# Stacked operands and values in a chunked RWKV-7 scan on one Trainium2 core

## The chip, the cores and the metric

The kernel runs on one core of one Trainium2 chip. The metric is the time of one execution on the device in microseconds (us); the median of the timed runs stands for a kernel. All data are float32.

## The reference

The program is a two-layer hybrid diffusion backbone: 256 latent and 256 context tokens of 1024 channels. Each layer has a Fourier mix, a latent attention, a bidirectional RWKV-7 recurrence, a gated merge, and a mixture of experts. The change concerns the recurrence alone:

```python
def wkv_scan(r, w, k, v, a, b, S0, reverse):
    def step(S, inp):
        rt, wt, kt, vt, at, bt = inp
        sa = jnp.einsum('bhvk,bhk->bhv', S, at)
        S = S * wt[:, :, None, :] + sa[..., None] * bt[:, :, None, :] + vt[..., None] * kt[:, :, None, :]
        return S, jnp.einsum('bhvk,bhk->bhv', S, rt)
...
    for d in range(2):
        ...
        s_fin, yd = wkv_scan(rh, decay, kd, vh, -kk, kk * a, S0[d], reverse=(d == 1))
        ys.append(yd)
...
y_ctx, s_ctx = rwkv_mix(pr_c, zero_state, *rw)
y_lat, _ = rwkv_mix(pr_l, s_ctx, *rw)
```

There are 8 heads of 64 channels and two directions d (0 forward, 1 backward). The context is scanned first, then the latent tokens from the context's last state. In the second (last) layer nobody reads the context's output y, only its state.

## The kernel before

**Layout.** Two heads share the 128 partitions (h = 0 in partitions 0 to 63, h = 1 in 64 to 127), and four such pairs j = 0 to 3 lie beside each other, so one head is a 64x64 block and one operand of a direction a 128x256 tile. PSUM has 8 banks of 128x512; the helper `part(d, n, x)` is half x of bank 4d+n.

**Steps.** A chunk is 64 tokens. A layer's scan has `STEPS` = 8 steps: k = 0 to 3 are the context, k = 4 to 7 the latent tokens, and each step handles one chunk of either direction. `streams(l, k)` says that y is wanted: always in layer 0, in layer 1 only for k of 4 and more. In a step a chunk's recurrence is a triangular system: `couple` makes its 64x64 matrix from keys and decays; `begin` masks it (MT) and starts the inverse X and its transpose XT with 2x2 blocks (negated neighbours plus the unit diagonal); five levels n = 0 to 4 double the blocks, each by `join` (BT times X into PSUM), a ScalarE copy to PS (L1254), `grow` (XT times PS), and on VectorE an add and a 32x32-block transpose (L1619, L1621). `grams` makes the masked score matrices Grb, Grk, Gak; `turns` transposes keys (Bt, Kt), `values` transposes the chunk's values (Vt), by products with an identity block.

**The chunk before.** What depends on the state runs one step late, between the pieces of the inverse: `correct(k-1)` makes the right-hand side, `solve(k-1)` U = X^T RHS, `readout(k-1)` the output, `update(k-1)` the new state.

**Order.** The order on each engine is written out by hand. TensorE in step k: couple(k), correct(k-1), grams(k, 0), solve(k-1), grams(k, 1), then the levels; turns(k) stand in level 0, readout(k-1) in levels 1 and 2, update(k-1) in level 3, values(k+1) in level 4. VectorE: begin and masks, the running sums of the decays for k+1 (`cumulate`), then per level the add and transpose of both directions, `operands(k+1, d)` in levels 1 and 2, `read` (y += readout) there too, `totals` and `update` in level 3. ScalarE copies PSUM to SBUF and takes the exponentials; GpSimd (POOL) multiplies MT by each level's mask (`blocks`, L1914) and subtracts and multiplies for the decays.

**Names.** L731 is the single matmul line of all scan products. L1590 is the last operand of `couple`; L1596 to L1600 are `begin`; L1607, L1608, L1611 the masks; L1624 the last add of level 4; L1639 and L1640 the state's add and its product with the total decay; L1220 the copy of the turned keys, L1225 of the values, L1230 of the right-hand side, L1235 of U. In the trace a float32 product of the program is two matmul records, a transpose through TensorE one.

The loop over the levels, on TensorE:

```python
for n in range(len(LEVELS)):
    join(k, n, 0)
    ...
    join(k, n, 1)
    ...
    grow(k, n, 0)
    grow(k, n, 1)
```

## Time and profile before

| | |
|---|---|
| Median of 3 runs | 2350.64 us (2346.11 to 2356.69) |
| The profiled execution's own time | 2349.85 us |
| Its span in the trace | 2348.2 us |
| TensorE busy | 2101.7 us (90%) |
| VectorE, ScalarE, GpSimd busy | 720.6, 487.9, 274.7 us |
| Scan of layer 0, first couple to last readout | 420.4 to 620.8 us |
| Scan of layer 1, the same | 1625 to 1819 us |
| Matmuls of L731 | 11520 records |

Busy time counts an engine as busy while any of its instructions is in flight. A scan matmul is in flight for some 0.22 us and the next begins long before it ends, so a busy TensorE can still have room; the distance between starts is the measure there. PEclk is the share of full clock that TensorE was granted: 1.00 is 2.4 GHz, 0.50 is 1.2 GHz.

### The profile page before, as it was taken

To read this page: it belongs to the slowest core of one execution; us is meant where nothing else is said; L and a number is where in the kernel's file an instruction comes from. 1 tells how busy PE (TensorE), PEld (TensorE's weight loads), DVE (VectorE), ACT (ScalarE), POOL (GpSimd) and SP (SyncE) were. 2 spreads that over 40 slices of the span, in tenths; PEclk is the share of its full clock that TensorE was granted. 3 is DMA by queue.
4 is the path that set the end of the run, shared out by engine and by line. 5 is a ranking of instruction groups with operands and counts; after the bars stand their busy time and mean duration, and the time that the engine had idled before them with its cause. 6 is when DMAs were issued, how large, how long until landed. Compare 5 with 4: busy or idle time off the path is not lost. (4 is left out here: it accounts for less than half of the span.)

```text
span 2348.2 us, 53901 instructions
## 1 busy us (share of the span) xinstructions
PE 2101.7 (90%) x23898; PEld 1349.7 (57%) x23898; DVE 720.6 (31%) x1768; ACT 487.9 (21%) x1120; POOL 274.7 (12%) x463
## 2 busy tenths in 40 slices
PE   6999899899899999999999789898999899987784
PEld 2454443889644444446556465554898788754442
DVE  1033334777431011310100032546676311200002
ACT  2123312333220000301111132323332301110011
POOL 0000000443100001101111100001343000011111
PEclk8999999899999999999999989998899999998996
DMA  7148716000121212448999821110000344799993
GB/s 287 61 154 344 305 65 226 3 4 4 56 90 54 108 54 108 181 161 328 398 383 395 306 90 51 69 50 1 4 4 4 146 159 188 274 378 397 395 406 122
DMA packets 55828, 399.91 MB, mean 170 GB/s; under 512 B 6672, under 2 KB 22928, under 8 KB 33648
## 3 DMA queue, kind: packets, MB, share of 16 engines
q1 hardware_dynamic: 43440, 361.94, 39.9%
q0 software_dynamic: 8576, 23.08, 2.6%
q10 hardware_dynamic: 3648, 12.45, 1.7%
q8 instruction: 134, 2.20, 0.4%
q14 instruction: 30, 0.25, 0.0%
HBM read 365.47 MB, written 31.98 MB: 169 GB/s over the span
## 5 line engine op out<-in xcount | busy, mean ns | idle before, releaser
L494 PE MATMUL ps<-H,memory 128*128 128x512 f32 (+2 forms) x1728 | 615.1, 512 | 11.6 <-DMA memory<-in_w_in 9.7
L494 PEld LDWEIGHTS ps<-H,memory 128*128 128x128 f32 (+1 forms) x1728 | 327.5, 190 | 286.5 <-issue 251.6
L731 PE MATMUL ps<-memory 64*64 64x32 f32 (+2 forms) x10112 | 329.0, 229 | 33.6 <-DVE memory L1624 10.1
L994 PE MATMUL ps<-memory 128*32 128x256 f32 x5120 | 298.8, 395 | 49.2 <-DMA memory<-in_eu 47.7
L731 PEld LDWEIGHTS ps<-memory 64*64 64x64 f32 x10112 | 316.4, 142 | 43.3 <-issue 21.3
L494 PE MATMUL ps<-memory 128*128 128x512 f32 (+3 forms) x928 | 319.2, 495 | 6.2 <-issue 3.0
L994 PEld LDWEIGHTS ps<-memory 128*32 128x32 f32 x5120 | 184.8, 114 | 160.0 <-issue 71.0
L494 PEld LDWEIGHTS ps<-memory 128*128 128x128 f32 (+1 forms) x928 | 173.8, 188 | 143.6 <-issue 127.3
L1019 PE MATMUL ps<-memory 128*32 128x256 f32 x2560 | 144.8, 380 | 5.0 <-ACT memory L1342 3.8
L1914 POOL TENSOR_TENSOR memory<-memory,cons 128x256 f32<-128x256 f32 x160 | 117.9, 752 | 122.5 <-DVE memory L1596 78.7
L1019 PEld LDWEIGHTS ps<-memory 128*32 128x32 f32 x2560 | 79.6, 110 | 59.9 <-ACT memory L1342 10.1
L1979 POOL DMA_DIRECT2D expert_rows<-memory x128 | 69.3, 542 | 299.1 <-DVE memory L1846 276.4
L1278 ACT ACTIVATE memory<-ps 128x512 f32<-128x512 f32 (+1 forms) x48 | 23.6, 491 | 329.3 <-PE ps L494 329.3
L1714 DVE TENSOR_TENSOR memory<-memory,ps 128x512 f32<-128x512 f32 (+1 forms) x32 | 17.8, 555 | 209.6 <-PE ps L494 209.6
L1254 ACT COPY memory<-ps 128x128 f32<-128x128 f32 x160 | 43.0, 269 | 173.2 <-PE ps L731 173.2
L731 PE MATMUL ps<-cons,memory 64*64 64x64 f32 x1408 | 59.2, 233 | 13.5 <-issue 10.5
L731 PEld LDWEIGHTS ps<-cons,memory 64*64 64x64 f32 x1408 | 52.0, 146 | 16.5 <-issue 12.2
L1841 DVE TENSOR_TENSOR memory<-memory,ps 128x256 f32<-128x256 f32 x16 | 6.7, 421 | 174.3 <-ACT memory L1340 174.3
L1619 DVE TENSOR_TENSOR memory<-memory,ps 128x128 f32<-128x128 f32 x128 | 34.4, 269 | 78.4 <-PE ps L731 78.2
L1621 DVE STREAM_TRANSPOSE memory<-memory 128x256 f32<-128x256 f32 x128 | 57.0, 445 | 4.4
L1846 DVE COPY memory<-ps 128x256 f32<-128x256 f32 x32 | 13.6, 424 | 137.8 <-PE ps L1019 137.8
L1952 POOL TENSOR_TENSOR memory<-H 128x512 f32<-128x512 f32 (+1 forms) x2 | 2.0, 993 | 436.1 <-ACT H L1288 436.1
(251 smaller groups left out, 1804.9 us busy)
## 6 DMA issues: line engine op xcount, KB each, us to landing
memory<-in_eg SPq DMA_DIRECT2D x32, 2048.0 KB, 17.2
memory<-in_eu SPq DMA_DIRECT2D x32, 2048.0 KB, 23.0
memory<-in_ed SPq DMA_DIRECT2D x32, 2048.0 KB, 23.4
memory<-in_w_ada SPq DMA_DIRECT2D x24, 2048.0 KB, 9.5
memory<-in_w_in SPq DMA_DIRECT2D x20, 2048.0 KB, 7.6
expert_rows<-memory SPq DMA_DIRECT2D x4, 3456.0 KB, 23.7
memory<-in_w_out SPq DMA_DIRECT2D x4, 2048.0 KB, 7.8
memory<-expert_rows ACTq DMA_DIRECT2D x19, 384.0 KB, 10.4
```

Of the source, the lines that this page charges most:

```text
L494: ins = mm(ps[0:M, bank, 0:w], lhs(k), rhs(k), start=(k == 0), stop=(k == n - 1))
L731: ins = mm(out[cols, j], lhs[rows, j, :], rhs[rows, j], start=(n == 0), stop=(n == len(terms) - 1))
L994: ins = mm(out_.rearrange("p (x n) -> p x n", x=2), XGT[:, k, g * GROUP:g * GROUP + GROUP], sets[b][:, 0:2, k * 512 + c * P:k * 512 + c * ...
L1019: ins = mm(ps[cc, 6 if last else 5, at:at + 256], HIDT[:, 0, g * P + k * GROUP:g * P + k * GROUP + GROUP], sets[b][:, 2, k * D + c * 256:k ...
L1254: act.copy(under(PS[n][d], n, d), under(part(d, 3, 0).rearrange("p (j n) -> p j n", n=CH), n, d))\
L1278: act.activation(SG[:, o % 2, 0:w], ps[:, 2 * (o % 2), 0:w], ACT.Sigmoid).then_inc(sem("merge_sigmoid"), 1)
L1619: tt(x, x, under(half(d, 2, 1 - p), n, d), ALU.add).then_inc(sem("inverse"), 1)
L1621: dve.transpose(flat(TWICE["XT"][p][d]), flat(ONCE["X"][d])).then_inc(sem("inverse"), 1)
L1714: link(tt(TM[:, 0, 0:w], gate, proj, ALU.mult))
L1846: dve.tensor_copy(YG[:, b, (groups - 1) * 256:groups * 256], ps[:, 6, 0:256]).then_inc(sem("result_copied"), 1)
L1914: tt(BTS[n][d], ONCE["MT"][d], over_pairs(con_(f"lev{LEVELS[n]}")), ALU.mult).then_inc(sem("blocks"), 1)
L1979: pool.dma_start(xg[bass.ds((2 * i + b) * tr, tr), c * 256:c * 256 + 256] .rearrange("(g t) n -> t g n", t=GROUP), YG[GROUP * c:GROUP * c ...
```

## The change

- **Stacked operands.** The two operands of the keys lie side by side per pair (`BB`), so that one matmul with 128 stationary columns makes what two made (`grams`), and one transpose turns both (`turns`). These are now true TensorE transposes, no longer products with an identity.
- **Stacked values.** U and the values V share one tile `UV` of 128 partitions (64 of U, 64 of V for each head), as do their score matrices (`GR`) and keys (`BK`). `readout` and `update` contract over 128 rows, and two products become one. V is transposed once for both directions (`pick`, `VC`).
- **Order.** `correct` is split in two; on TensorE `solve` now stands behind grams(k, 1), the turns move to level 1, both readouts to level 2, both updates stand together in level 3, and the values behind the levels. Bank numbers change (`bank`).
- **ScalarE** takes over three things: it writes the unit diagonal into XT a step ahead (`diagonals`), so that VectorE's begin is a mask, a predicated copy and a transpose; it multiplies the state by the total decay in four pieces of 128x64 per direction (`decayed_state`); it copies y at the first visit of a chunk (`first_read`), so that GpSimd no longer zeroes Y. Signs are moved (`B` is negated at its making) so that no copy has to negate.

```diff
+        GR = [[pairs(piece(2)) for d in range(2)] for p in range(2)]
+        UV = [pairs(piece(2)) for d in range(2)]
+        BB = [pairs(piece(2)) for d in range(2)]
+        GAK = pairs(piece(2))
+        VC = pairs(piece(2))
...
+                def values(k):
+                    pe.wait_ge(sem("values_moved"), picked(l * STEPS + k))
...
+                            ins = pe.transpose(ps[:, bank(h, 3), 256 + CH * j:256 + CH * j + CH], VC[side(h), j], eye[side(h), :])
...
                 def grams(k, d):
...
-                    pe.wait_ge(sem("values_held"), nth(N, d))
+                    if k:
+                        pe.wait_ge(sem("state"), states(l, k - 1, d))
...
+                            ins = mm(ps[:, bank(d, h), 128 * j:128 * j + CH * wide], BB[d][side(h), j], ER[p][d][side(h), 0:wide, j],
+                                     start=True, stop=True)
...
+                            ins = pe.transpose(ps[:, bank(d, h), CH * j:CH * j + CH], BB[d][side(h), j], eye[side(h), :])
...
+                def correct_values(k):
+                    N = l * STEPS + k
+                    for d in both:
+                        pe.wait_ge(sem("masked"), nth(N, d))
+                        pe.wait_ge(sem("values_moved"), held(N, d))
...
+                    for j, d, h in problems:
+                        mm(part(d, 1, 0)[side(h), j], ONCE["S"][d][side(h), j], ER[p][d][side(h), 1, j], start=(j == 0), stop=False)
+                    for j, d, h in problems:
+                        ins = mm(part(d, 1, 0)[side(h), j], UV[d][:, j, h], GR[p][d][:, j, h], start=False, stop=(j == RJ - 1))
...
                     if n == 0 and k:
-                        pe.wait_ge(sem("u_copied"), nth(N - 1, d))
+                        pe.wait_ge(sem("u_copied"), nth(N - 1, 1))
...
                 def solve(k):
                     for d in range(2):
                         act.wait_ge(sem("u"), nth(l * STEPS + k, d))
-                        act.copy(flat(ONCE["U"][d]), part(d, 3, 1)).then_inc(sem("u_copied"), 1)
+                        rows = side(d)
+                        act.copy(by_head(UV[d])[rows], quarters(rows, slice(bank(0, 3), bank(1, 3) + 1), 1)[:, ::-1 if d else 1]).then_inc(sem("u_copied"), 1)
+
+                def diagonals(k):
+
+                    for d in range(2):
+                        act.copy(TWICE["XT"][k % 2][d], over_pairs(con_("eye")))
...
+                def decayed_state(k, d):
+
+                    act.wait_ge(sem("state_added"), carried(l, k, d))
+                    for j in range(RJ):
+                        x = ONCE["S"][d][:, j]
+                        ins = act.activation(x, x, ACT.Identity, scale=total[:, k % 3, d, j:j + 1])
+                    ins.then_inc(sem("state"), 1)
...
-                    link(tt(turned, half(d, 2, p), over_pairs(con_(f"pair{1 - d}")), ALU.mult))
-                    link(tt(turned, turned, over_pairs(con_("eye")), ALU.add))
+                    dve.wait_ge(sem("exps"), grown(N, d))
+                    link(dve.copy_predicated(turned, over_pairs(con_(f"pair{1 - d}")).bitcast(mybir.dt.uint32), half(d, 2, p)))
...
-                    link(tt(state, state, half(d, 0, 0), ALU.add))
-                    tt(state, state, total[:, k % 3, d, :].unsqueeze(2).broadcast_to([P, RJ, CH]), ALU.mult)\
-                        .then_inc(sem("state"), 1)
+                    tt(state, state, half(d, 0, 0), ALU.add).then_inc(sem("state_added"), 1)
...
-                pool.memset(Y[:, :, :], 0.0)
```

The front of a step on TensorE, before. Rows are matmuls of the program, output shape behind the names; the 64x2x64 rows are the wide half of grams, and the last row is join(k, 0, 0).

```order
L731 MATMUL ps<-memory 64x64 [waits keys,inverse]
L731 MATMUL ps<-memory 64x64 x15
L731 MATMUL ps<-memory 64x64 [waits state,masked,values_held]
L731 MATMUL ps<-memory 64x64 x31
L731 MATMUL ps<-memory 64x64 [waits queries,read,values_held]
L731 MATMUL ps<-memory 64x64 x7
L731 MATMUL ps<-memory 64x2x64 x8
L731 MATMUL ps<-memory 64x64 [waits rhs_copied,inverse]
L731 MATMUL ps<-memory 64x64 x15
L731 MATMUL ps<-memory 64x64 [waits queries,read,values_held]
L731 MATMUL ps<-memory 64x64 x7
L731 MATMUL ps<-memory 64x2x64 x8
```

Behind them stands join(k, 0, 0), which waits for u_copied, inverse and blocks. The same place in the changed kernel (L775 couple, L817 and L827 the two halves of correct, L800 grams, L838 solve, L875 join):

```order
L775 MATMUL ps<-memory 64x64 x15
L817 MATMUL ps<-memory 64x64 [waits masked,values_moved]
L817 MATMUL ps<-memory 64x64 x15
L800 MATMUL ps<-memory 128x128 [waits queries,read,state]
L800 MATMUL ps<-memory 128x128 x7
L827 MATMUL ps<-memory 64x64 [waits state,values]
L827 MATMUL ps<-memory 64x64 x15
L800 MATMUL ps<-memory 128x128 [waits queries,read,state]
L800 MATMUL ps<-memory 128x128 x7
L838 MATMUL ps<-memory 64x64 [waits rhs_copied,inverse]
L838 MATMUL ps<-memory 64x64 x15
L875 MATMUL ps<-memory 64x16x2 [waits u_copied,inverse,blocks]
```

Solve moved behind the second grams and now touches the join that waits for its copy, and the product after couple now waits for copied values.

ScalarE from the end of level 4 into the next step, before (L1254 level copies, L1225 values, L1230 right-hand side, L1197 log decays, L1235 U):

```order
L1254 COPY memory<-ps 128x4x32 [waits joined] x2
L1225 COPY memory<-ps 128x256 [waits values] x2
L1230 ACTIVATE memory<-ps 128x256 [waits rhs] x2
L1197 COPY memory<-memory 128x256 [waits rhs] x2
L1235 COPY memory<-ps 128x256 [waits u] x2
```

And in the changed kernel (L1357 level copies, L1333 the decayed state, L1305 values, L1316 U, L1321 the diagonals):

```order
L1357 COPY memory<-ps 128x4x32 [waits joined] x2
L1333 ACTIVATE memory<-memory,total 128x64 [waits state_added]
L1333 ACTIVATE memory<-memory,total 128x64 x3
L1333 ACTIVATE memory<-memory,total 128x64 [waits state_added]
L1333 ACTIVATE memory<-memory,total 128x64 x3
L1305 COPY memory<-ps 64x2x4x64 [waits values]
L1305 COPY memory<-ps 64x2x4x64
L1310 COPY memory<-ps 128x256 [waits rhs] x2
L1265 COPY memory<-memory 128x256 [waits rhs] x2
L1316 COPY memory<-ps 64x2x4x64 [waits u] x2
L1321 COPY memory<-cons 128x256 x2
```

Eight small activations now stand ahead of the values' copies, and those copies and U's have 512 elements per partition, on 64 partitions, where they had 256 on 128.

## Rows read from the trace of the kernel before

**Rows 1.** The page, part 1: busy us (share of the span), instructions.
```profile
PE 2101.7 (90%) x23898; PEld 1349.7 (57%) x23898; DVE 720.6 (31%) x1768; ACT 487.9 (21%) x1120; POOL 274.7 (12%) x463
```

**Rows 2.** Windows, one scan step each; columns are named in the first row.
```profile
core 0: us, PE busy (x) PEld busy (x) DVE busy (x) ACT busy (x) POOL busy (x), PEclk, DMA share, GB/s
442.50:466.50 24.00, 22.78 (x768) 22.36 (x769) 18.01 (x48) 8.11 (x26) 10.21 (x14) 1.00 0.02 5
...
541.50:567.00 25.50, 22.84 (x768) 22.41 (x769) 18.21 (x48) 8.11 (x26) 10.21 (x14) 1.00 0.02 5
591.10:612.40 21.30, 20.30 (x672) 19.65 (x673) 13.65 (x38) 3.99 (x14) 7.37 (x11) 0.99 0.02 4
1649.70:1674.30 24.60, 22.94 (x640) 22.17 (x641) 16.78 (x42) 8.12 (x26) 8.80 (x12) 0.79 0.01 4
1674.30:1695.90 21.60, 19.07 (x644) 18.16 (x645) 16.80 (x42) 8.10 (x26) 8.80 (x12) 1.00 0.02 4
1744.00:1768.00 24.00, 22.73 (x781) 22.24 (x781) 17.98 (x48) 8.10 (x26) 10.21 (x14) 1.00 0.02 4
```

**Rows 3.** Windows of L731 alone: a couple, and a level without other work.
```profile
567.02:567.50 0.48, 0.48 (x31) 0.48 (x33) 1.00 0.00 0
1682.74:1685.17 2.43, 2.43 (x64) 2.24 (x65) 1.00 0.02 7
```

**Rows 4.** Timeline of TensorE at three places: start us, us, what, [idle before].
```profile
499.68 1.15 PE L731 MATMUL ps<-cons,memory 64*64 64x64 f32 x32 [0.26 <-issue]
...
164.82 0.66 PE L668 MATMUL ps<-cons,memory 128*128 128x128 f32 x4
165.41 1.09 PE L649 MATMUL ps<-memory 128*64 128x128 f32 x8
...
982.17 2.30 PE L941 MATMUL ps<-memory,cons 128*128 128x16 f32 x20
```

**Rows 5.** Groups of ScalarE by form: out<-in xcount | busy us, mean ns | idle before.
```profile
L1220 ACT COPY memory<-ps 128x512 f32<-128x512 f32 x28 | 16.4, 586 | 26.1 <-PE ps L731 26.1
...
L1225 ACT COPY memory<-ps 128x256 f32<-128x256 f32 x32 | 11.0, 373 | 0.7 <-PE ps L731 0.7
...
L1303 ACT ACTIVATE memory<-ps 128x64 f32<-128x64 f32 x1 | 0.2, 242 | 0.0
```

**Rows 6.** Groups of VectorE by form.
```profile
L1599 DVE TENSOR_TENSOR memory<-memory,cons 128x256 f32<-128x256 f32 x32 | 23.1, 722 | 1.1
L1640 DVE TENSOR_TENSOR memory<-memory,total 128x256 f32<-128x256 f32 x28 | 18.0, 642 | 1.0
...
L1598 DVE TENSOR_TENSOR memory<-ps,cons 128x256 f32<-128x256 f32 x32 | 13.1, 410 | 0.0
...
L1639 DVE TENSOR_TENSOR memory<-memory,ps 128x256 f32<-128x256 f32 x28 | 11.4, 407 | 0.0
...
L1714 DVE TENSOR_TENSOR memory<-memory,ps 128x512 f32<-128x512 f32 x16 | 11.0, 688 | 140.3 <-PE ps L494 140.3
```

**Rows 7.** Timeline of VectorE and TensorE, end of one step and the next couple.
```profile
589.81 0.73 DVE L1640 TENSOR_TENSOR memory<-memory,total 128x256 f32<-128x256 f32 x1
590.47 0.47 DVE L1624 TENSOR_TENSOR memory<-memory,ps 128x128 f32<-128x128 f32 x2
...
591.08 0.33 PE L731 MATMUL ps<-memory 64*64 64x64 f32 x6 [0.84 <-DVE memory L1624]
```

**Rows 8.** Windows around two falls of TensorE's clock.
```profile
1639.50:1642.90 3.40, 2.88 (x91) 2.71 (x87) 3.33 (x10) 1.06 (x4) 1.92 (x4) 1.00 0.02 5
1642.90:1649.70 6.80, 6.32 (x124) 6.21 (x120) 2.47 (x10) 1.23 (x5) 0.00 (x0) 0.50 0.01 2
...
1707.80:1711.20 3.40, 2.29 (x76) 2.30 (x74) 3.33 (x9) 0.85 (x3) 1.08 (x2) 1.00 0.00 0
1711.20:1714.60 3.40, 3.40 (x72) 3.40 (x69) 0.60 (x2) 0.27 (x1) 0.00 (x0) 0.50 0.03 7
```

**Rows 9.** The zeroing of Y, from the groups of GpSimd.
```profile
L1897 POOL MEMSET memory<- 128x2048 f32 x2 | 3.6, 1804 | 227.2 <-DVE marks L1376 227.2
```

More of the change, by code:

```diff
@@ L766, in turns @@
+                    ins.then_inc(sem("grams"), 1)
                 def turns(k, d):
                     pe.wait_ge(sem("masked"), nth(l * STEPS + k, d))
-                    heads(None, (part(d, 0, 0), (ONCE["bE2"][d], eye, 0, 0)))
-                    heads("turns", (part(d, 0, 1), (ONCE["bKk"][d], eye, 0, 0)))
-                def correct(k):
+                    for j in range(RJ):
+                        for h in both:
+                            ins = pe.transpose(ps[:, bank(d, h), CH * j:CH * j + CH], BB[d][side(h), j], eye[side(h), :])
@@ new lines, in update @@
+                def update(k):
+                    N, p = l * STEPS + k, k % 2
+                    for d in both:
+                        pe.wait_ge(sem("u_copied"), nth(N, d))
+                        pe.wait_ge(sem("masked"), nth(N + 1, d))
+                        if k + 2 < STEPS:
+                            pe.wait_ge(sem("turned"), carried(l, k + 1, d))
+                    for j, d, h in problems:
+                        ins = mm(part(d, 0, 0)[side(h), j], BK[p][d][:, j, h], UV[d][:, j, h], start=True, stop=True)
+                        if j == RJ - 1 and h:
+                            ins.then_inc(sem("step"), 1)
@@ L804, in join, with heads @@
+                def heads(signal, made, lhs, rhs, d):
+                    for j in range(RJ):
+                        for h in both:
+                            at = side(h ^ d)
+                            ins = mm(made[at, j], lhs[at, j], rhs[at, j], start=True, stop=True)
+                    ins.then_inc(sem(signal), 1)
                 def join(k, n, d):
@@ L1240, in _ @@
                     growths(0, d)
+                for d in range(2):
                     decays(0, d)
-                values(0)
                 for k in range(STEPS):
@@ L1250, in _ @@
                         solve(k - 1)
+                        if more:
+                            diagonals(k + 1)
                     for n in range(len(LEVELS)):
@@ L1255, in _ @@
                                .then_inc(sem("joined_copied"), 1)
-                            if n == 0 and more:
+                        if more and n == 1:
+                            for d in range(2):
                                 turns(k, d)
-                        if more and n in (1, 2):
-                            decays(k + 1, n - 1)
                         if more and n < 2:
@@ L1262, in _ @@
                             growths(k + 1, n)
-                    if more:
-                        values(k + 1)
+                        if more and n == 2:
+                            for d in range(2):
+                                decays(k + 1, d)
+                        if n == 2:
+                            pick(k)
+                        if n == 3 and k and first(k - 1) and streams(l, k - 1):
+                            for d in range(2):
+                                first_read(k - 1, d)
+                    if k:
+                        for d in range(2):
+                            decayed_state(k - 1, d)
+                    values(k)
                 correct(STEPS - 1)
@@ L1626, in read @@
                 def read(k, d):
-                    if streams(l, k):
+                    if streams(l, k) and not first(k):
                         dve.wait_ge(sem("readout"), 2 * readouts(l, k) - 1 + d)
```

221 lines of the change are left out of this document (123 added, 98 removed).

## The prediction

> **What bounds the kernel now.** I read the busy shares first: TensorE is in flight 90% of the span, no other engine over 31% [rows 1]. The change touches the scan alone, so I cut it into steps [rows 2]. A middle step of layer 0 takes 24.0 to 25.5 us; its six middle steps fill 442.5 to 591.1 us, 24.8 us each. They hold 768 matmuls, 18 us of VectorE, 8 of ScalarE, 10 of GpSimd. TensorE sets the end, though "busy" hides how full it is, so I price its matmuls by the distance between starts.
>
> - Where the blocks lie on the array's diagonal (h stays h: levels, readout, update), two run at a time: 32 products in 1.15 us, 0.22 of it the last one's flight, so 29 ns each [rows 4].
> - Where all four quarters are used (couple, correct, solve), 31 take 0.48 us: 15 ns [rows 3].
> - Loading 128 stationary columns sets 107 ns even when 16 columns are streamed: 20 in 2.30 us with 0.26 of flight [rows 4]. Two such on different row halves make 53 ns. The wide scores of before also stream 128 columns, 53 ns.
>
> Before, a full step has 128 records at 15 ns (1.9 us), 32 wide ones at 53 ns (1.7) and 608 at 29 ns (17.6): 21.2 us. So 3.6 us of 24.8 are waits: a level's own chain (64 records are 1.87 us, an unfilled level takes 2.43 [rows 3]) and the end of the step, where couple waits 0.84 us for VectorE's last add, which itself starts only after the state's product [rows 7].
>
> **What TensorE loses in work.** After, a full step has 128 records at 15 ns (1.9 us), 32 scores with 128 stationary columns at 53 ns (1.7), levels, readout and update 320 + 64 + 32 = 416 at 29 ns (12.1), and 24 transposes, one record each, which I take at 29 ns (0.7; bounds 15 and 53 ns, 0.4 to 1.3 us). That is 16.4 us, 4.8 less. If only that counted, 14 steps would give over 55 us. In layer 1, k = 0 to 3, there is no readout and the scores were narrow (32 at 29 ns, now 53): the work falls by only some 2.2 us.
>
> **What VectorE loses.** The diagonal's add (722 ns) goes, the masked product (410) becomes a predicated copy whose price no row shows; from 0.41 to 0.72 us, I take 0.41 [rows 6]. The state's product (642 ns) goes to ScalarE. Masks become one operation of 512 elements (688) for two of 256 (about 410 each), but Gak is also 512 now. Two directions together: about 3 us less of 18. This shortens the step's end, since the last add stands behind the state's product no more: 1.2 us there [rows 7]. At the front it gives slack only.
>
> **What is hidden or free.** The diagonals (ScalarE, 2 of 256 elements, near L1225's 373 ns [rows 5]) lie between U's copy and the first level copy, which waits for a join anyway; without that cover they would cost 0.7 us a step. The first reads move 0.4 us from VectorE to ScalarE. Y's zeroing was 1.8 us twice on GpSimd while TensorE made projections: nothing [rows 9].
>
> **The new waits**, in a full step, from couple = 0:
>
> 1. *Values.* The product behind couple now needs the copied values. On ScalarE eight activations of 128x64 (242 ns alone [rows 5]; in a row I take 0.16, between 0.10 and 0.24) stand ahead of two copies of 512 elements (586 ns each, 1.1 together [rows 5]). They can't begin before the state's adds and the last level copy, about 1.1 us before couple. The copies are done at 1.3 + 1.1 - 1.1 = 1.3 us, plus 0.15 of signals; couple ends at 0.5. TensorE stands 0.95 us, and scores, solve and the first join are queued behind.
> 2. *U.* Solve is now the last thing before join(k, 0, 0), which waits for both copies of U: 0.22 of flight, 1.1 for two copies of 512, 0.1 of signals: 1.4 us. Before, grams(k, 1), 1.2 us, stood there and hid copies of 373 ns.
> 3. *Shape changes.* Where the tile shape on the array changes, the next matmul starts 0.07 us before the previous ends, not 0.16 or more: L668 starts at 164.82 and lasts 0.66, L649 follows at 165.41 [rows 4]. Scan matmuls fly 0.22 us, so a change costs 0.15 - 0.03 = 0.12 us. Before, all were 64x64. Now a step changes 12 times (scores, turns, readout, update, values), 10 of them on the path: 1.2 us (0 if such short ones don't wait, 1.8 at the outside).
>    The Trainium skill, page "TensorEngine Tiling (Array Packing)", section "Tiling Modes", says that changing the mode drains the engine; the rows agree, and by it no change would be free.
> 4. *Levels.* With less to fill them, levels 0 and 4 wait 0.55 us each for the copy and the add, the others 0.25: 1.9 us.
> 5. *The end.* Couple still waits about 0.6 us for the last adds.
>
> Sum of a full step: 16.4 + 0.95 + 1.4 + 1.2 + 1.9 + 0.6 = 22.5 us. Against 24.8 that is -2.3 for each of six steps, -13.8. In layer 1, 24.0 to 22.5 for k = 5 and 6 [rows 2] with fronts like these: -2.8; k = 4 lacks a readout, -1.2. For k = 1 to 3 the 21.6 us of a step at full clock [rows 2] become 21.2: -1.2. The first steps have no chunk before, so neither copy is waited for: -2. The last step (21.3 [rows 2]) and what follows it keep both waits and lose only readout and update work; I get +1.3 for each layer: +2.6. Together **-18.4 us at equal clock**.
>
> **The clock.** It fell from 1.00 to 0.50 after stretches with little in them: 87 weight loads and about as many matmuls in 3.4 us, or 74 [rows 8], all of them levels without filling, in steps without readout; never in a full step of layer 0. What a low stretch costs: the step of 24.6 us at 0.79 against 21.6 at 1.00 [rows 2], 3.0 us for 0.21 x 24.6 x 2 = 10 us of half clock, 0.3 us per us. In the changed kernel the stretch from solve to the end of level 0 holds 64 level matmuls in about 3.9 us, thinner than any of those. I take one fall in every second of nine full steps, 6.8 us long (as 1642.9 to 1649.7): 4.5 x 6.8 x 0.3 = 9 us. Bounds: none, or in every step, 20 us.
>
> By themselves, the transposes: the Trainium skill, page "TensorE: Matmul & The Clock Gate", section "Part 4: PE-mode transpose", says that transposes do not count as activity for the clock as matmuls do. If so, turning the keys does not fill level 1, and falls come more often; no row here shows it apart, since the clock stood at 1.00 through L668.
>
> **The forecast.** 2349.85 (the profiled execution's own time, 0.8 below the median) - 18.4 + 9 = 2340 us, -0.45% against the median. It lies on the border of what can be told from no change (0.5%, 12 us).
>
> **Rivals.**
>
> - *A, the work saved arrives* (chance 0.25). Shape changes are hidden in short matmuls, ScalarE's small activations overlap and the clock holds: 1.2 us less per step in 12 steps, values 0.4 earlier: -18.4 - 14 - 5 = -37, 2312 us. For it: TensorE's distances are the surest rows. Against: the U copy and values wait remain.
> - *B, the forecast* (0.40): 2325 to 2350, one fall in two steps.
> - *C, the waits eat it* (0.15). No new mechanism, the sizes at their upper ends: 0.24 us per small activation (+0.6), 53 ns per transpose, VectorE's operands for the next chunk held up by GpSimd in the emptier levels (0.4 a step): +1.2 in 12 steps, 2354 us: no change.
> - *D, the clock gives it back* (0.20). The thin stretch drops the clock in every step, and at half clock levels reach only 58 ns a matmul, so it stays down until the readout or beyond, 10 us a step: 14 x 10 x 0.3 = 42 us instead of 9: 2373 us, slower. It decides from about 7 us of half clock per step on; for it stand all falls of before, which came in such stretches; against it, that full steps with 1 us of standstill before couple never fell.
> - *The change does not do what it says*: the order of rows shows the merged matmuls, so this can only be the predicated copy costing over 1 us each; VectorE has 1.5 us of slack at the front, so even then under 0.5 us a step.
>
> **How the numbers follow.** A lies wholly under 2339; of B nearly half does (0.18). Faster by over 0.5%: 0.25 + 0.18 = 0.43. B's rest and most of C are within 0.5%: 0.22 + 0.13 = 0.35. D and C's tail: 0.22 slower. The range from A's centre to beyond B and C, 2312 to 2368, leaves out half of A's low side and the upper half of D, 2 in 10. The likeliest case alone has 2325 to 2350.
>
> **What would show it.** In the profile after: scan records down from 11520 to about 9000; 53 ns between grams records; an idle of about 0.9 us before correct_values (released by L1305) and 1.4 us before the first join of each step (released by L1316); starts 0.15 us apart at the edges of grams, turns, readout, update; no wait for the state's product before couple; middle steps of 22 to 23 us where PEclk is 1.00. More than two stretches of PEclk 0.50 in three steps say D; steps under 21.5 us say A. I am wrong at the root if steps at full clock stay at 24.8 us, or if VectorE or ScalarE releases TensorE inside the levels for over 1 us a level.

## The result

| | before | after |
|---|---|---|
| Median | 2351.33 us (4 runs) | 2407.66 us (4 runs, 2400.68 to 2416.39) |
| Profiled execution | 2349.85 us | 2416.39 us |
| Its span, mean granted clock | 2348.2 us, 0.954 | 2414.7 us, 0.902 |
| Time at half clock, 2 x (1 - mean clock) x span | 216 us | 473 us |

The ratio is 1.0241, 95% interval 1.0200 to 1.0282: slower by 56 us, where 11 us less was forecast, and outside the range. The direction is that of rival D, and so is the clock as the cause; the loss is larger than D's own price, and D's thin stretch is only one of the places where the clock falls.

The profiled execution is the slowest of the four. By the spans and clocks of all four the kernel after has 451 us at half clock on average; the kernel before has 232 to 244, in the batches that were run beside the experiments.

Most of it lies in the two scans, first couple to last readout:

| | before | after |
|---|---|---|
| Scan of layer 0: us, PEclk | 200.4, 0.96 | 221.6, 0.78 |
| Scan of layer 1: us, PEclk | 194.0, 0.90 | 242.3, 0.59 |
| At half clock, both | some 55 us | some 295 us |

The page of the kernel after, part 1, against [rows 1]:

```profile
PE 2157.0 (89%) x21626; PEld 1387.5 (57%) x21626; DVE 696.7 (29%) x1672; ACT 553.3 (23%) x1292; POOL 269.6 (11%) x461
```

TensorE has 2272 matmul records fewer and is in flight 55 us longer. Windows of the kernel after, each from one couple to the next (columns as in [rows 2]):

```profile
470.55:494.90 24.35, 21.50 (x600) 20.01 (x601) 15.88 (x40) 12.66 (x41) 10.02 (x14) 0.93 0.01 4
494.90:525.09 30.19, 26.84 (x601) 25.13 (x601) 16.77 (x42) 12.36 (x39) 10.12 (x14) 0.72 0.01 2
...
1666.03:1696.95 30.92, 29.25 (x538) 27.91 (x536) 15.08 (x38) 12.22 (x37) 8.74 (x12) 0.50 0.01 2
```

The first two rows are steps of layer 0 with the same work. The one at 0.93 has 3.4 us of half clock, the one at 0.72 has 16.9 us, and is 5.84 us longer: 0.43 us for each us at half clock. Without its 3.4 us the first would take 22.9 us, against 24.8 before and 22.5 forecast. So at full clock the change works nearly as forecast. The last row is a step of layer 1 wholly at half clock; three such stand in a row, where [rows 2] has 21.6 us at 1.00. They are part of one stretch of 129.7 us at half clock. It begins at 1633.1 us, 9 us ahead of this scan's first couple, where TensorE has no matmul at all; the kernel before has a fall of 20.5 us there too, and its clock came back.

Timeline of TensorE after, one step of layer 0 (the columns of [rows 4]):

```profile
530.17 0.87 PE L827 MATMUL ps<-memory 64*64 64x64 f32 x32
530.97 1.16 PE L800 MATMUL ps<-memory 64*128 64x128 f32 x16
532.07 0.69 PE L838 MATMUL ps<-memory 64*64 64x64 f32 x32
534.12 2.81 PE L875 MATMUL ps<-memory 64*64 64x32 f32 x80 [1.36 <-ACT memory L1316]
536.87 0.71 PE L808 MATMUL ps<-cons,memory 64*128 64x64 f32 x16
...
549.95 0.69 PE L775 MATMUL ps<-memory 64*64 64x64 f32 x32 [0.60 <-DVE memory L1737]
551.98 0.81 PE L817 MATMUL ps<-memory 64*64 64x64 f32 x20 [1.33 <-ACT memory L1305]
```

Both new waits are where the forecast put them: ahead of correct_values (L817, released by the values' copies L1305) and ahead of the first join (L875, released by U's copies L1316). Over both layers TensorE stands 19.2 us behind L1316 and 16.8 us behind L1305:

```profile
L875 PE MATMUL ps<-memory 64*64 64x32 f32 x5120 | 231.0, 255 | 20.4 <-ACT memory L1316 19.2
```

```profile
L817 PE MATMUL ps<-memory 64*64 64x64 f32 x512 | 17.7, 310 | 16.8 <-ACT memory L1305 16.8
```

The forecast had 0.95 + 1.4 = 2.35 us a step for the two, between starts; they take 1.55 + 1.58 = 3.13 us. In 14 steps that is 11 us of a miss of 67, and some of it was won back elsewhere in the step (see the terms below). The clock is the rest. Windows around two falls in layer 0:

```profile
523.40:526.80 3.40, 1.79 (x62) 1.50 (x58) 2.50 (x8) 3.00 (x10) 1.94 (x3) 1.00 0.02 5
526.80:530.20 3.40, 3.08 (x52) 2.77 (x52) 1.37 (x4) 0.18 (x1) 2.35 (x4) 0.56 0.00 0
...
557.50:560.90 3.40, 2.04 (x68) 1.77 (x65) 2.26 (x4) 1.98 (x5) 1.51 (x3) 0.94 0.02 5
560.90:571.20 10.30, 10.30 (x193) 9.99 (x191) 4.45 (x11) 3.45 (x11) 3.57 (x5) 0.52 0.01 2
```

The first pair is the end of a step, the couple (525.09) and the values' wait: TensorE is in flight 1.79 of 3.40 us, and then the clock is at 0.56. Each of the five middle steps from 470.55 on, and the last one, has its first fall 1.1 to 2.3 us behind its couple. In two of them, as in the second pair, a further fall of 10 us follows the wait for U (here behind the solve of 558.04 us). Before, no full step of layer 0 had one.

The first step of a layer is different. No chunk stands before it, so it waits neither for the values' copies nor for U's, and it falls all the same. The first row is this step before; the others are two stretches of it after, and the stretch at 0.50 goes on for 20.5 us:

```profile
420.40:442.50 22.10, 20.72 (x512) 19.92 (x513) 15.28 (x43) 6.36 (x21) 12.26 (x18) 0.83 0.02 3
...
424.80:428.20 3.40, 2.57 (x72) 2.32 (x70) 3.33 (x7) 1.27 (x4) 1.60 (x3) 1.00 0.02 5
428.20:444.17 15.97, 15.61 (x281) 15.28 (x281) 8.87 (x27) 4.85 (x15) 6.95 (x11) 0.50 0.01 3
```

```profile
428.56 1.07 PE L875 MATMUL ps<-memory 64*64 64x32 f32 x16 [1.19 <-DVE memory L1732]
```

It takes 23.4 us with 409 records, where 512 took 22.1. What changed here is level 0: the turns stood in it before and stand in level 1 now, so TensorE idles 1.19 us in it for VectorE's add (last row). No run puts the turns back alone, so that they hold the clock there is likely but not shown.

### The profile page after: what moved, and what is told of

Read it like the earlier page. It is cut to its first block and busy times, and to the rows that moved or that the text cites. A ratio compares the mean times of both kernels' runs of the same rounds, so it can differ in the third digit from the quotient of the medians.

```text
span 2414.7 us, 49410 instructions
## 1 busy us (share of the span) xinstructions
PE 2157.0 (89%) x21626; PEld 1387.5 (57%) x21626; DVE 696.7 (29%) x1672; ACT 553.3 (23%) x1292; POOL 269.6 (11%) x461
## 5 line engine op out<-in xcount | busy, mean ns | idle before, releaser
L875 PE MATMUL ps<-memory 64*64 64x32 f32 x5120 | 231.0, 255 | 20.4 <-ACT memory L1316 19.2
L875 PEld LDWEIGHTS ps<-memory 64*64 64x64 f32 x5120 | 222.5, 177 | 28.2 <-issue 22.2
L1357 ACT COPY memory<-ps 128x128 f32<-128x128 f32 x160 | 42.9, 268 | 185.9 <-PE ps L875 185.1
L800 PE MATMUL ps<-memory 64*128 64x128 f32 (+1 forms) x512 | 56.3, 388 | 0.0
L556 PE MATMUL ps<-memory 128*32 128x512 f32 x384 | 47.3, 615 | 4.9 <-DMA memory<-in_w_ada 4.5
L800 PEld LDWEIGHTS ps<-memory 64*128 64x128 f32 x512 | 49.5, 286 | 3.1
## 6 DMA issues: line engine op xcount, KB each, us to landing
memory<-in_ed SPq DMA_DIRECT2D x32, 2048.0 KB, 22.8
memory<-expert_rows ACTq DMA_DIRECT2D x19, 384.0 KB, 10.2
```

The lines of the kernel that those rows point to most:

```text
L556: ins = mm(ps[32 * g:32 * g + 32, bank, :], CP[:, k, at:at + 32], slot(n, "ADA")[:, k * 512:k * 512 + 512], start=(n == first and k < 4), ...
L800: ins = mm(ps[:, bank(d, h), 128 * j:128 * j + CH * wide], BB[d][side(h), j], ER[p][d][side(h), 0:wide, j], start=True, stop=True)
L875: ins = mm(made[at, j], lhs[at, j], rhs[at, j], start=True, stop=True)
L1357: act.copy(under(PS[n][d], n, d), under(part(d, 3, 0).rearrange("p (j n) -> p j n", n=CH), n, d))\
```

## The experiments

"At half clock" is 2 x (1 - mean clock) x span: of the profiled execution, as above, and then the mean over all timed executions of that kernel. A profile is a single execution, so 20 us more or less between two profiles say little, and the mean is the better measure. Ratios are against the kernel before on the same chip.

| Kernel | Median us | Ratio, 95% interval | At half clock | Mean |
|---|---|---|---|---|
| solve ahead of grams(k, 1) | 2405.72 | 1.0234 (1.0184 to 1.0284) | 447 | 451 |
| values copied ahead of the state | 2411.32 | 1.0240 (1.0188 to 1.0292) | 482 | 477 |
| products for transposes | 2450.22 | 1.0412 (1.0368 to 1.0457) | 465 | 480 |
| both waits filled | 2374.73 | 1.0104 (1.0044 to 1.0164) | 299 | 299 |
| the values' wait filled | 2415.21 | 1.0255 (1.0195 to 1.0316) | 444 | 432 |
| work put back | 2434.62 | 1.0346 (1.0287 to 1.0405) | 386 | 369 |
| kernel before, solve late | 2358.77 | 1.0019 (0.9994 to 1.0044) | 236 | 236 |
| fitted fillings | 2371.18 | 1.0061 (1.0042 to 1.0080) | 284 | 298 |
| early grams, fillings | 2349.53 | 0.9982 (0.9958 to 1.0007) | 311 | 285 |
| the same, state on VectorE | 2377.52 | 1.0080 (1.0051 to 1.0109) | 337 | 326 |
| after, state on VectorE | 2402.80 | 1.0204 (1.0166 to 1.0242) | 427 | 451 |
| early grams, more filling | 2355.87 | 1.0020 (0.9998 to 1.0042) | 292 | 289 |

**Solve ahead of grams(k, 1).** This is the order of before, which hid the copies of U.

```diff
-                    grams(k, 1)
                     if k:
                         solve(k - 1)
+                    grams(k, 1)
```

> The changed kernel with solve put back between grams(k, 0)/correct_state and grams(k, 1), so that the copies of U lie under grams(k, 1). Rival (waits by themselves): the 1.6 us before the first join shrink to 0.3, but the right-hand side's copies (0.9 us) are no longer covered: 0.3 us a step, 2400 to 2408. Theory 1 (clock): one long standstill becomes two short ones, fewer falls, 2375 to 2400.

Windows of two steps of layer 0:

```profile
467.22:490.01 22.79, 20.12 (x601) 18.74 (x601) 15.88 (x40) 12.65 (x41) 9.94 (x14) 1.00 0.01 4
514.74:545.26 30.52, 27.66 (x601) 25.95 (x601) 16.77 (x42) 12.30 (x38) 10.04 (x14) 0.66 0.01 2
```

The same 601 matmuls take 22.79 us at 1.00 and 30.52 us at 0.66. A step of this kernel can beat the 24.8 us of before by 2 us, and the kernel is 2.3% slower all the same. The timeline of its TensorE shows where the waits are now:

```profile
469.29 0.69 PE L817 MATMUL ps<-memory 64*64 64x64 f32 x32 [1.38 <-ACT memory L1305]
...
472.64 0.69 PE L838 MATMUL ps<-memory 64*64 64x64 f32 x32 [0.94 <-ACT memory L1310]
...
474.69 1.50 PE L875 MATMUL ps<-memory 64*64 64x32 f32 x42 [0.26 <-ACT memory L1316]
```

The wait for U shrank from 1.36 to 0.26 us, and solve waits 0.94 us for its right-hand side instead. The values' wait is untouched, and the clock did not come back. Every fall in the middle steps of layer 0 (3.4 or 20.5 us) begins 1.1 to 2.0 us behind couple, where the values' wait lies, and none behind the first join. The time is in the rival's interval, though its reason (the waits by their length alone) does not explain the step at 1.00.

**Values copied ahead of the state's product** on ScalarE (the eight activations of decayed_state now follow values(k)).

```diff
-                    if k:
-                        for d in range(2):
-                            decayed_state(k - 1, d)
                     values(k)
+                    if k:
+                        for d in range(2):
+                            decayed_state(k - 1, d)
```

> The changed kernel with ScalarE's copies of the values ahead of the state's eight small activations. The product behind couple then waits 0.4 us and not 1.4; correct_state waits some 0.3 us for the state. Rival (waits by themselves): 1.0 us in 14 steps, 2390 to 2396 us. Theory 1 (clock): over twice that, 2350 to 2385, with less half-clock time in the scans.

Timeline of its TensorE:

```profile
578.02 0.69 PE L775 MATMUL ps<-memory 64*64 64x64 f32 x32
579.31 0.69 PE L817 MATMUL ps<-memory 64*64 64x64 f32 x32 [0.59 <-ACT memory L1305]
580.19 1.16 PE L800 MATMUL ps<-memory 64*128 64x128 f32 x16 [0.19 <-ACT memory L1333]
```

The values' wait fell from 1.33 to 0.59 us, a part of it came back as a wait for the state (0.19), and the half-clock time stayed. But the falls moved: in layer 0's middle steps they begin 8.4 to 9.9 us behind couple now, at the wait for U, and none is left behind couple. Neither theory's interval held; the shorter wait bought no time, because the falls at the other wait (6.8 to 27.3 us long) are no shorter than those that went.

**Ordinary products for the transposes** (keys and values; `mm` with the identity block in place of `pe.transpose`), for the theory that transposes don't fill TensorE as far as the clock is concerned.

```diff
-                            ins = pe.transpose(ps[:, bank(d, h), CH * j:CH * j + CH], BB[d][side(h), j], eye[side(h), :])
+                            ins = mm(ps[:, bank(d, h), CH * j:CH * j + CH], BB[d][side(h), j], eye[side(h), :],
+                                     start=True, stop=True)
```

> The changed kernel with the keys' and values' transposes as ordinary products with the identity (two records each, 24 records more a step, 0.7 us more work). If transposes do not count as activity for the clock and that is what lets it fall: 2360 to 2395 us, and less half-clock time. If they count or do not matter: 2405 to 2420 us.

Windows of it, to be set beside 30.92 us at 0.50 and 24.35 us at 0.93 after:

```profile
474.63:500.33 25.70, 23.43 (x626) 21.98 (x624) 15.88 (x40) 12.69 (x41) 10.01 (x14) 0.93 0.02 4
...
1718.56:1753.32 34.76, 33.08 (x562) 31.75 (x560) 15.06 (x38) 12.25 (x37) 8.73 (x12) 0.50 0.01 2
```

24 records more in a step: 1.35 us more with little half clock, and 3.84 us more at half clock. In 16 steps that is between 22 and 61 us, so the added work is enough to explain the 42 us. The half-clock time did not fall (465 us against 473; means 480 and 451), so the theory is out: that the turns and values are transposes is not what brings the clock down here.

**Both waits filled.** Solve ahead of grams(k, 1), and products of 128x128 by 256 columns ahead of the two waits: 4 ahead of the values', 3 ahead of solve's. They write a bank that nobody reads at that time, and nothing uses what they make.

```diff
+                def fill(count, k):
...
+                    for n in range(count):
+                        mm(ps[:, 3, 0:256], ident, con_("reset", RJ * CH), start=True, stop=True)
...
                     if k:
+                        fill(4, k)
                         correct_values(k - 1)
...
+                        fill(3, k)
                         solve(k - 1)
+                    grams(k, 1)
```

> The changed kernel with the solve put ahead of the second direction's grams (which alone gave 2405.7 us), and in each full step 4 products of 128x128 by 256 columns ahead of the values' wait and 3 more ahead of the wait of the solve, into a bank that nobody reads then; nothing reads what they make. Theory 1 (the step's standstills and lighter products let the granted clock fall, and the half clock is what costs): half-clock time falls from 451 us to under 280, steps of 23 to 24.5 us, 2335 to 2370 us. Rival (the clock falls for something that filled waits don't touch): the products that outlast the waits come on top, at half clock above all, 2405 to 2440 us, half-clock time over 400 us.

Windows of a middle step of layer 0 and of a stretch of layer 1 in which the clock fell, then the timeline of one front:

```profile
473.91:497.67 23.76, 23.40 (x614) 21.17 (x615) 15.89 (x40) 12.66 (x41) 9.94 (x14) 1.00 0.01 4
...
1664.00:1691.90 27.90, 26.60 (x559) 24.11 (x555) 14.73 (x40) 12.14 (x38) 8.66 (x12) 0.76 0.01 3
```

```profile
521.93 0.69 PE L775 MATMUL ps<-memory 64*64 64x64 f32 x32 [0.60 <-DVE memory L1746]
522.56 1.99 PE L900 MATMUL ps<-cons 128*128 128x256 f32 x8
524.48 0.69 PE L817 MATMUL ps<-memory 64*64 64x64 f32 x32
```

No middle step of layer 0 fell any more, and work that has no use made the kernel 31 us faster than the same order without it. This run shows that what happens at the two waits brings the clock down in these steps. It does not say whether the idle time or the missing work matters there, since a filling ends the one and adds the other. It ends 5 us above the interval, with 299 us at half clock instead of under 280. Apart from the ends of the scans, three places keep their falls: the first step of layer 0 (20.5 us, as in the changed kernel), a stretch of 34.1 us that starts ahead of layer 1's scan and covers its first step, and two falls of 13.7 us in the steps behind it, which have no readout and the narrow grams. The fillings also outlast their wait: from the end of couple to L817 it is 1.9 us where it was 1.33.

**Only the values' wait filled** (4 products, the order of the changed kernel).

```diff
                     if k:
+                        fill(4, k)
                         correct_values(k - 1)
```

> The changed kernel with only the 4 products ahead of the values' wait, and the order of the step untouched. Theory 1: one of the two long standstills is gone, so part of the half-clock time goes, 2355 to 2400 us. Rival: 2405 to 2430 us. If both fillings are needed, this one stays near 2407 us and the one with both does not.

```profile
480.60 3.79 PE L875 MATMUL ps<-memory 64*64 64x32 f32 x80 [1.36 <-ACT memory L1324]
```

```profile
481.90:492.10 10.20, 10.20 (x190) 9.90 (x190) 4.45 (x11) 3.15 (x10) 3.65 (x6) 0.51 0.01 3
```

The first row is the join behind the wait for U, the second the window that follows it. The falls behind the couple are gone from layer 0, but one of 10.2 us right behind the wait for U stands in four of its six middle steps. The time is that of the expectation's last sentence: near the changed kernel. With the values' wait filled, the standstill for U is enough to make the clock fall, as the values' wait was in the first experiment, where U's had shrunk to 0.26 us.

**Work put back**: couple, grams, solve and update are issued twice, with the same values into the same places. The wait for U stays as it was, but the second couple covers half of the values' wait.

```diff
                     for j, d, h in problems:
+                        mm(part(d, 0, 0)[side(h), j], BK[p][d][:, j, h], UV[d][:, j, h], start=True, stop=True)
+                    for j, d, h in problems:
                         ins = mm(part(d, 0, 0)[side(h), j], BK[p][d][:, j, h], UV[d][:, j, h], start=True, stop=True)
```

> The changed kernel with couplings, grams, solve and update issued twice each (the same values into the same places): about 3.5 us of TensorE's work come back at full clock, 3.0 us of it on the path, and the standstills stay as long as they are. If the work taken out is what let the clock fall: half-clock time back under 280 us, and 2407 - 57 + 14 x 3.0 = about 2390 us (2375 to 2405). If the standstills themselves are what does it, or neither: half-clock time over 400 us and 2445 to 2480 us.

Timeline of the two waits, then windows of two middle steps of layer 0:

```profile
479.98 0.69 PE L819 MATMUL ps<-memory 64*64 64x64 f32 x32 [0.66 <-ACT memory L1311]
...
487.72 3.29 PE L881 MATMUL ps<-memory 64*64 64x32 f32 x80 [1.36 <-ACT memory L1322]
```

```profile
477.90:508.01 30.11, 28.00 (x729) 26.52 (x729) 16.19 (x40) 12.75 (x41) 10.10 (x14) 0.83 0.01 4
570.92:597.29 26.37, 23.95 (x729) 22.46 (x729) 15.77 (x40) 12.60 (x40) 10.06 (x14) 1.00 0.02 4
```

Between the two: 729 matmuls a step, nearly as many as before (768), and still 386 us at half clock. The work put back takes some 85 us of half clock away (the 130 us in a row of layer 1 are 41), but it does not hold the clock. In layer 0 four of the five middle steps from 477.90 us on still fall, each 11.5 to 12.6 us behind couple, at the wait for U; one, the second row, does not. So a standstill of 1.36 us usually brings the clock down even in a nearly full step.

**The kernel before with its solve behind grams(k, 1)**, the other half of that question: all its products, and a standstill for U.

```diff
+                    grams(k, 1)
                     if k:
                         solve(k - 1)
-                    grams(k, 1)
```

> The kernel before with one thing of the changed order: the solve stands behind the second direction's grams, so that TensorE waits for ScalarE's copies of U with nothing issued. If a standstill of some 1 us in a step is enough to bring the clock down in a kernel that has all its products: half-clock time over 350 us and 2375 us or more. If the clock needs the lighter step too: half-clock time 210 to 270 us and only the wait, 14 x 0.3 to 1.2 us, 2355 to 2368 us.

Timeline of TensorE, then the window of a step of layer 0:

```profile
509.04 0.66 PE L731 MATMUL ps<-memory 64*64 64x32 f32 x16 [0.55 <-ACT memory L1235]
```

```profile
481.99:507.94 25.95, 23.12 (x749) 22.29 (x752) 17.96 (x50) 8.10 (x26) 10.19 (x14) 1.00 0.02 4
```

The standstill is there (0.55 us behind the copy of U, L1235) and the clock stays at 1.00. It is shorter than the 1.36 us of the changed kernel, since the copies are shorter (two of 256 elements), and level 0 behind it is filled with the turns. A standstill of this size in a full step costs at most some 6 us by the medians (0.4 us a step), with 1 inside the ratio's interval. Time and half-clock time are in the second interval, that of a clock that needs the lighter step too.

**Fitted fillings**: 3 products ahead of the values, 2 ahead of solve, and 2 at level 2 in layer 1 where the readout is missing.

```diff
                         if n == 2 and k and streams(l, k - 1):
                             readout(k - 1)
+                        elif n == 2 and k and more:
...
+                            fill(2, k)
```

> The kernel with both fillings (2374.7 us), with the fillings cut to the waits that they cover (3 products instead of 4 ahead of the values, 2 instead of 3 ahead of the solve, each 0.43 us), and 2 products where the second layer's first steps have no readout. Theory 1: steps at full clock of 24.0 - 0.8 = 23.2 us, and the falls of the second layer's first half (50 us at half clock there) mostly gone: 14 x 0.8 + 40 x 0.22 = 20 us less, 2350 to 2362 us. If the fillings were only just enough, the falls come back and it stays at 2365 to 2395 us.

```profile
469.73:492.84 23.11, 22.75 (x611) 20.59 (x611) 15.94 (x40) 12.65 (x41) 9.94 (x14) 1.00 0.02 4
```

The steps came out as worked out (23.1 against 23.2 us), the time did not: 2371 us, within the second interval, with as much half-clock time as with both waits filled (means 298 and 299 us). In layer 1's first half the two falls of 13.7 us became one of 23.9 us in another step.

**Early grams**: useful work in the place of two of the fillings.

```diff
                     couple(k)
+                    grams(k, 0)
                     if k:
+                        fill(1, k)
                         correct_values(k - 1)
-                    grams(k, 0)
...
                         correct_state(k - 1)
+                        fill(2, k)
+                        solve(k - 1)
```

> As the one with the fitted fillings, but the first direction's grams are issued ahead of the values' wait, in place of two of its products: useful work covers the wait, and the chain to U is shorter by their 0.83 us. Theory 1: steps of 22.4 to 22.9 us at full clock, 2335 to 2352 us, at or below the kernel before. Rival: grams fill the wait less densely, the falls come back, 2360 to 2400 us.

```profile
466.63:488.93 22.30, 21.85 (x606) 19.76 (x607) 15.80 (x40) 12.64 (x41) 9.94 (x14) 1.00 0.02 4
...
1671.29:1692.48 21.19, 20.72 (x547) 18.45 (x547) 14.17 (x38) 12.09 (x39) 8.54 (x12) 1.00 0.01 3
1713.85:1742.17 28.32, 27.96 (x546) 25.11 (x546) 16.19 (x40) 12.93 (x41) 10.00 (x14) 0.67 0.01 2
```

```profile
488.93 0.69 PE L775 MATMUL ps<-memory 64*64 64x64 f32 x32
489.56 1.16 PE L800 MATMUL ps<-memory 64*128 64x128 f32 x16
490.65 0.70 PE L900 MATMUL ps<-cons 128*128 128x256 f32 x2
491.28 0.70 PE L817 MATMUL ps<-memory 64*64 64x64 f32 x32
```

58 us faster than the changed kernel, and level with the kernel before: the interval of the ratio holds 1. Its steps at full clock are 2.5 us shorter than those of before; the half clock (third row: 28.32 us at 0.67) takes that away again. The profiled execution, 9 us above the median, has 95 us more of it than that of before; by the means of the timed executions it is 285 against 244 us, 41 more. Within the 12 timed executions of this kernel the time follows the half clock, from 2341.0 us with 267 to 2365.6 us with 331.

**The same with the state's product back on VectorE.**

```diff
-                    tt(state, state, half(d, 0, 0), ALU.add).then_inc(sem("state_added"), 1)
+                    link(tt(state, state, half(d, 0, 0), ALU.add))
+                    tt(state, state, total[:, k % 3, d, :].unsqueeze(2).broadcast_to([P, RJ, CH]), ALU.mult)\
+                        .then_inc(sem("state"), 1)
```

> As the one with early grams, with the state's product with its decays back on VectorE, as in the kernel before (2 products a step of about 0.4 us in place of ScalarE's eight small operations of 2.0 us). If the 2.0 us ahead of the values' copies are what the wait is made of: TensorE waits about 0.7 us less a step for the values, 2325 to 2345 us. If VectorE is as near the bound, its 0.7 us a step come on top of the levels: 2345 to 2360 us.

```profile
524.59 0.73 DVE L1762 TENSOR_TENSOR memory<-memory,total 128x256 f32<-128x256 f32 x1
525.24 0.47 DVE L1746 TENSOR_TENSOR memory<-memory,ps 128x128 f32<-128x128 f32 x2
```

```profile
525.86 1.08 PE L775 MATMUL ps<-memory 64*64 64x64 f32 x32 [1.69 <-DVE memory L1746]
```

28 us slower than with ScalarE's activations, and above both intervals. The last add of level 4 (L1746) stands behind the second of two products of 0.73 us, and couple waits 1.69 us for it, where it did not wait in the run above (488.93). The clock falls in each of the five middle steps from 474.86 us on, within 1.3 us of couple. In this order the move to ScalarE is worth its time, by somewhat more than the forecast's "1.2 us there".

**The changed kernel with only that.**

> The changed kernel with only the state's product back on VectorE, nothing filled. Theory 1 (what matters is how thin the step is, and the values' wait is one of two standstills): half-clock time 300 to 450 us, 2370 to 2400 us. Rival (the eight small operations of ScalarE are the whole harm): at or under the kernel before, 2330 to 2355 us. If VectorE pays as much as ScalarE saves: 2405 to 2425 us.

```profile
488.89 0.69 PE L775 MATMUL ps<-memory 64*64 64x64 f32 x32 [1.11 <-DVE memory L1734]
489.37 0.99 PE L817 MATMUL ps<-memory 64*64 64x64 f32 x32
...
496.35 0.85 PE L875 MATMUL ps<-memory 64*64 64x32 f32 x23 [1.36 <-ACT memory L1316]
```

2402.80 us lies between the first and the third interval, with 427 us at half clock and the same mean as the changed kernel, 451 us. The values' wait is gone, couple waits 1.11 us instead of 0.60, and the wait for U is what it was, 1.36 us. The eight small operations are not the whole harm, which was the rival; the standstill that they made moved in part to couple.

**Early grams with 4 products in place of 2** in layer 1.

> As the kernel with early grams (2349.5 us), with 4 products in place of 2 where the second layer's first steps have no readout. Theory 1: the fall of 24 us at 1724 us, in the middle of the second layer, goes (24 x 0.25 = 6 us), for 3 x 0.86 = 2.6 us of products: 2343 to 2350 us. If the fall has another place than the missing readout, it stays, and the products come on top: 2350 to 2358 us.

In the interval of the second case. The fall of 23.9 us is gone, but three shorter ones (6.8, 10.2 and 6.8 us) stand in three steps in a row. Nothing was gained: layer 1's scan is at 0.82 with either filling, 202.9 us long with 2 products and 206.8 us with 4, and the means are 285 and 289 us at half clock. Where in layer 1's first half more work would hold the clock was not found.

## Why the prediction was wrong

**The terms of the step were nearly right.** Measured against forecast, at full clock:

- TensorE's work: 9248 records in the two scans (2272 fewer, 11520 before). 16 grams in 1.16 us; turns 16 in 0.71 us, 33 ns each after 0.22 of flight (forecast 29). A change of shape: L800 starts 0.07 us before L827 ends (530.97 against 531.04), as forecast from [rows 4].
- Predicated copy: 431 ns (0.41 taken). The copies of 512 elements: 580 ns (586 taken). VectorE is busy 15.9 us in a full step, 2.1 less than before (3 taken).
- The values' wait: 1.33 us of idle, 1.55 between starts, 0.95 forecast. The eight activations took 2.02 us, 0.25 each, just above the bounds of 0.10 to 0.24, where 0.16 was taken. They start 1.35 us before couple, not 1.1.
- The wait for U: 1.58 us between starts, 1.4 forecast. Couple's wait: 0.60 us, as forecast.

Groups by form of layer 0's scan after, for two of these:

```profile
L1333 ACT ACTIVATE memory<-memory,total 128x64 f32<-128x64 f32 x56 | 14.1, 337 | 1.0 <-DVE memory L1752 1.0
```

```profile
L1709 DVE COPY_PREDICATED memory<-cons,ps 128x256 f32<-128x256 uint32 x16 | 6.9, 431 | 0.0
```

A step takes 22.9 us instead of 22.5, less than the two waits alone would add (0.78 us). The 0.4 us, in about 12 steps, turn -18.4 us at equal clock into an estimate of -13. Two sums of the forecast are off without weight in it: k = 5 and 6 at 1.5 us each are -3.0, not -2.8, and the terms of rival C (0.6 + 0.6 + 0.4) are 1.6 us a step, not 1.2, so C's time would be 2359 us.

**The step that failed is the clock**: "I take one fall in every second of nine full steps, 6.8 us long", 31 us at half clock for 9 us of time. There were 257 us more in the profiled execution, some 240 of them in the scans. The nine full steps have 118 us at half clock, the first four steps of layer 1 116 us, the first step of layer 0 20 us. Three things in it were wrong:

1. *Which stretch is thin.* The forecast looked from solve to the end of level 0. Eight steps of the 16 have a fall there, 10.1 to 12.3 us behind couple. But in layer 0 the first falls come elsewhere: at the end of a step and across the values' wait, where two standstills (0.60 and 1.33 us) lie on either side of a couple that needs 0.5 us. In 3.4 us of it 62 matmuls were started; ahead of the falls of [rows 8] it was 91 and 76. The forecast had both waits in its own list (1 and 5), without adding them up.
2. *That a fall ends by itself.* In layer 1 the clock was at 0.50 for three whole steps in a row, with TensorE in flight for 29.25 of 30.92 us. Those steps were given 21.2 us each and no fall, and the first steps of both layers were given none either.
3. *D's chance was too low.* D was to decide from about 7 us of half clock a step, and the nine full steps have 13 us on average. The argument against D was that full steps with 1 us of standstill never fell. They had one such standstill, the changed step has three.

The price per us was right: 66.5 us between the profiled executions and some 13 gained make 80 us for 257, 0.31 against 0.3. (By the medians, 56 us, and the means of the timed executions it is 0.33; between two steps of layer 0 it was 0.43.)

**The cause**, as far as it is shown. In the steps with a chunk before them, TensorE's standstills at the values' and U's copies, with less work around them, let the granted clock fall. Filling both, with nothing else changed against the same order, ended the falls of layer 0's middle steps and gave back 31 us. With only the values' wait filled the falls stand at U's wait (2415 us), and with U's wait shrunk to 0.26 us they stand at the values' (2406 us, with 0.94 us of idle ahead of solve beside it): one long standstill in a step is enough. The work put back, with U's wait kept, gave back some 85 us at half clock, the two fillings some 150, so both count. A filling ends idle time and adds work at once, and no run parts the two. The waits' own length is the smaller part. In the full step of before, one standstill was tried only at 0.55 us.

The first step of layer 0 is a second, smaller cause: it has neither wait, but a level 0 without the turns, and has 20 us at half clock where it had 7. Which part of that lets the clock fall was not tried.

**Open**: what would hold the clock in the first step of either layer and in the steps of layer 1 behind it, which fall in every variant of the changed kernel. No filling was tried in a first step. Fillings at level 2 moved the falls and did not end them; fillings inside other levels were not tried.

## What to carry to other kernels

Price a change on TensorE at full clock and at half clock, and add up the standstills of a step, those on either side of a short piece of work above all: work taken off the engine around them can cost more than it saves. Put useful work that is ready (here grams) ahead of an instruction that waits for a copy; where there is none, a product into a free bank that nobody reads can pay. Compare steps at the same granted clock before you judge an edit: here the same 601 matmuls took 22.8 or 30.5 us. And compare the clock over all timed executions, since a single profile can lie 20 us off their mean.

## What the runs showed of the hardware

- TensorE stayed at 1.2 GHz (0.50) for 129.7 us, through three steps with matmuls in flight 29.25 of 30.92 us.
- A product of 128x128 by 256 columns is two records, 0.23 us from start to start of a record (8 records in 1.99 us, 0.38 of flight off the last). Eight scaled activations of 128x64 in a row on ScalarE, each in place, take 0.25 us each.
- A TensorE transpose of 64 rows by 128 columns costs about 33 ns (one record); as a float32 product with the identity block it is two records, and 48 of them in place of 24 made a step wholly at half clock 3.84 us longer. The page "TensorE: Matmul & The Clock Gate" of the Trainium skill, section "Part 4: PE-mode transpose", would have the products hold the clock better, since it says that the clock does not treat transposes as work in the same way. No run here shows that: with the products the half-clock time was 465 us, against 473.
